# Six of the twelve pairs of layer-1 modulation tiles moved from the prompt attention into the first group of the sample attention

## The reference, cut to what matters

```python
def adaln(c, w, b):
    m = jax.nn.silu(c) @ w + b          # w: 1024 x 6144 per layer
    m = m.reshape(c.shape[0], 1, 6, D_MODEL)
    return [m[:, :, k] for k in range(6)]

def mla_sample(h, past_lat, past_rope, w_in, q_g, kv_g, w_qb, w_kvb, w_o):
...
    k_lat = jnp.concatenate([past_lat, ckv], axis=1)      # pages gathered by page_table
    k_pe = jnp.concatenate([past_rope, kr], axis=1)
    q = jnp.concatenate([q_lat, q_pe], axis=-1)
    k = jnp.concatenate([k_lat, k_pe], axis=-1)[:, :, None, :]
    o_lat = causal_attention(q, k, k_lat[:, :, None, :], t0)
```

## Time and profile before

| | before |
|---|---|
| median of 3 runs | 1791.84 us (1791.68 to 1793.46) |
| profiled execution: its own time, its span | 1792.22 us, 1790.4 us |
| TensorE busy; mean granted clock | 1670.3 us (93%); 0.966 |
| VectorE, ScalarE, GpSimd busy | 450.0, 266.8, 93.8 us |
| moved by DMA | 457.07 MB, mean 255 GB/s |
| prompt attention, first to last turning of probabilities | 177.35 to 252.57 us |
| sample attention, first cache transposition to output projection | 256.88 to 350.06 us |

### The profile page before, as it was taken

One profiled execution on the slowest core, in us unless ns is written; L12 is line 12 of the kernel. 1 busy time (PEld: TensorE's weight loads), 2 busy tenths in 40 slices (PEclk: granted clock), 3 DMA queues, 4 the chain that ended last, 5 costly groups with the idle time before them and its releaser, 6 DMA issues.

```text
span 1790.4 us, 21220 instructions
## 1 busy us (share of the span) xinstructions
PE 1670.3 (93%) x8202; PEld 1065.9 (60%) x8202; DVE 450.0 (25%) x1128; ACT 266.8 (15%) x564; POOL 93.8 (5%) x173
## 2 busy tenths in 40 slices
PE   6999997799999999987997999999999999999996
PEld 4555553478888878766774454554445544554454
DVE  2233432220000055698466000020000200020002
ACT  2222222110000022333312000010001000100002
POOL 0001415000000010100000000000000000000000
PEclk9998998899999999998998999999999999999998
DMA  9755963244434554544476699999999899989993
GB/s 339 263 205 170 335 227 109 82 130 142 153 111 129 184 187 123 146 130 125 134 285 239 229 360 390 385 360 363 380 385 382 294 383 392 383 301 369 383 387 139
DMA packets 253068, 457.07 MB, mean 255 GB/s; under 512 B 12959, under 2 KB 112316, under 8 KB 249861
## 3 DMA queue, kind: packets, MB, share of 16 engines
q1 hardware_dynamic: 240640, 413.03, 65.5%
q0 software_dynamic: 10224, 41.71, 6.7%
q10 hardware_dynamic: 2112, 1.05, 0.2%
HBM read 443.54 MB, written 12.40 MB: 255 GB/s over the span
## 4 chain that ended last, share of the span: by engine, by line
PE 84%; DVE 8%; DMA 3%; issue 2%; ACT 1%; SPq 1%; POOLq 0%; POOL 0%; DVEq 0%; ACTq 0%
PE bank L1261 17%; PE bank L974 9%; PE bank L1300 9%; PE bank L1276 9%; PE bank L947 7%; PE bank L1312 4%; PE bank L988 4%; PE bank L687 2%; DMA st<-in_state_ssm 2%; PE bank L1022 1%; PE bank L777 1%; PE bank L724 1%; DVE ysp L1907 1%; PE bank L695 1%; DVE prod L1906 1%
## 5 line engine op out<-in xcount | busy, mean ns | idle before, releaser
L1261 PE MATMUL bank<-ring,hg 128*128 128x512 f32 (+1 forms) x624 | 255.1, 566 | 0.0
L1261 PEld LDWEIGHTS bank<-ring,hg 128*128 128x128 f32 x624 | 118.7, 192 | 129.2 <-issue 126.7
L974 PE MATMUL bank<-hT,ring 128*128 128x264 f32 x704 | 156.9, 386 | 1.3 <-ACT hT L1397 1.3
L974 PEld LDWEIGHTS bank<-hT,ring 128*128 128x128 f32 x704 | 133.7, 190 | 24.9 <-issue 2.1
L947 PE MATMUL bank<-hT,ring 128*128 128x264 f32 x512 | 117.4, 390 | 1.7 <-ACT hT L1397 1.3
L1300 PE MATMUL bank<-ring,turnH 128*128 128x512 f32 x256 | 114.4, 599 | 2.7 <-ACT turnH L1610 2.7
L947 PEld LDWEIGHTS bank<-hT,ring 128*128 128x128 f32 x512 | 98.1, 192 | 19.6 <-issue 2.1
L2172 DVE TENSOR_TENSOR actH<-sgH,bank 128x512 f32<-128x512 f32 (+1 forms) x24 | 15.4, 641 | 374.2 <-PE bank L1261 374.2
L1276 PE MATMUL bank<-ringx,hg 128*64 128x256 f32 x832 | 93.0, 381 | 0.0
L1300 PEld LDWEIGHTS bank<-ring,turnH 128*128 128x128 f32 x256 | 47.2, 190 | 67.3 <-issue 63.6
L988 PE MATMUL bank<-actT,ring 128*128 128x264 f32 x352 | 79.1, 386 | 0.6 <-DVE actT L1810 0.6
(11 more groups left out here) (483 smaller groups left out, 1945.5 us busy)
## 6 DMA issues: line engine op xcount, KB each, us to landing
ring<-in_moe_w_down SPq DMA_DIRECT2D x70, 1024.0 KB, 10.6
ring<-in_moe_w_up SPq DMA_DIRECT2D x59, 1024.0 KB, 8.1
ring<-in_moe_w_gate SPq DMA_DIRECT2D x55, 1024.0 KB, 8.8
ring<-in_w_ada SPq DMA_DIRECT2D x48, 1024.0 KB, 8.5
ringx<-in_moe_w_gate SPq DMA_DIRECT2D x37, 1024.0 KB, 7.9
ringx<-in_moe_w_up SPq DMA_DIRECT2D x33, 1024.0 KB, 10.0
ring<-in_ssm_w_in SPq DMA_DIRECT2D x20, 1024.0 KB, 5.4
ringx<-in_moe_w_down SPq DMA_DIRECT2D x20, 1024.0 KB, 10.0
```

What stands on the lines that cost most here:

```text
L974: m = mm(bank[2 * w + q][:, 0:T], slot8(tl)[:, k, q * P:(q + 1) * P], hT[:, k, :], start=k == 0, stop=k == DC - 1)
L1261: m = mm(bank[b_][:, 0:width], hg[:, k, 0:CAPH], w[:, kk, :], start=k == 0, stop=k == DC - 1)
```

## The change

`ada1_pairs` spreads six pairs over the sixteen heads in place of twelve: heads 2, 5, 7, 10, 13 and 15 now have one. The pairs 6 to 11 are computed in the first group of samples by `ada1_late`, in sequences 0, 1 and 2, one behind the second and one behind the fourth set of latent transpositions. The last turning, and TensorE's wait for the addition into `mod`, stand behind sequence 3's transpositions, and VectorE's copies and its addition move accordingly. The scores against a sample's own key, 8 columns of `bank[2]`, move to columns 432 to 439, beside the modulation that is now still in that bank.

```diff
+ADA1_EARLY = 6
 def ada1_pairs(h):
-    return range(h * 12 // H, (h + 1) * 12 // H)
+    return range(h * ADA1_EARLY // H, (h + 1) * ADA1_EARLY // H)
...
-        ada1_turn(11)
         values(H - 1)
...
         pe.wait_ge(s["o_copied"], H // 2)
-        pe.wait_ge(s["ada_added"], 4)
+        def ada1_late(p):
+            ada1_turn(p - 1)
+            ada_partials(ADA1 + 2 * p, bank[3], 12 + p + (1 if p == ADA1_EARLY else 2))
...
                     m.then_inc(s["lat_turned"], 1)
+                    if b < 3 and n % 2:
+                        ada1_late(ADA1_EARLY + 2 * b + n // 2)
...
                     m.then_inc(s["rope_turned"], 1)
+                if b == 3:
+                    ada1_turn(11)
+                    pe.wait_ge(s["ada_added"], 4)
...
-                            out = bank[half][rows, 0:512] if half < 2 else bank[2][rows, 0:NB]
+                            out = bank[half][rows, 0:512] if half < 2 else bank[2][rows, 432:432 + NB]
...
-        v.wait_ge(s["ada_turned"], 24)
-        ada_add(1, bank[2][:, 0:432], 0, 48, 4)
...
+                if b < 3:
+                    for p in (ADA1_EARLY + 2 * b, ADA1_EARLY + 2 * b + 1):
+                        v.wait_ge(s["units"], unit(ADA1 + 2 * p + 1))
+                        v.tensor_copy(adaS[:, p % 2, :], bank[3][:]).then_inc(s["ada_copied"], 1)
...
+                if b == 3:
+                    v.wait_ge(s["ada_turned"], 24)
+                    ada_add(1, bank[2][:, 0:432], 0, 48, 4)
...
-            link(v.tensor_tensor(s8[:], bank[2][:, 0:NB], cst[:, C_SMASK + NB * g_:C_SMASK + NB * (g_ + 1)], ALU.add))
+            link(v.tensor_tensor(s8[:], bank[2][:, 432:432 + NB], cst[:, C_SMASK + NB * g_:C_SMASK + NB * (g_ + 1)], ALU.add))
```

## The result

The changed kernel is slower: 1821.53 us, the median of four runs (1817.56 to 1822.92), against 1792.16 for the kernel before; the ratio is 1.0155, with a 95% interval from 1.0138 to 1.0173, which is +27.8 us. The forecast was +18.2. Its profiled execution took 1821.71 us, 29.5 more than that of before.

A forecast was written before the change was run, and what follows sets the result against it. TensorE was taken as the bound, 84% of the chain. Prompt attention -6.0, first group +11.6, page wait +10.6 and cold clock +2.0 sum to +18.2 us: 1810.0 against the median, range 1802 to 1820.

The forecast's parts named there:

- the clock falling after head 3: Prompt attention: a sign of being wrong; the clock was to stay at 1.00 from head 3 on.
- The other two signs: Signs of being wrong: a wait before sequence 5 under 6 or over 14 us, or TensorE waiting for `w_ada` tiles.
- The first group, +11.6: Sequences 0 to 3: six pairs add 15.9 us, covered waits and low clock take off 5.5, the last turning adds 1.2.
- The pages, +10.6: Before sequence 5: page loops start after the late 24th turning, SyncE needs 34.5 us, so TensorE waits 10.6 us.
- The cold clock behind the wait, +2.0: Sequence 5: TensorE is cold after the page wait, costing 1.4 to 3.8 us, taken as 2.0.
- the sample attention as a whole: Sample attention: the first group, the page wait and the cold clock after it, forecast together at +24.2 us.
- The prompt attention, -6.0: Prompt attention: +0.5 for heads 0 to 2, -4.9 for five heads, -1.0 last turning, -0.6 addition into `mod`.
- the term of five heads, -4.9: Heads 2 to 15: five heads lose their pair, each lasting 4.24 in place of 5.22 us.
- The rival of the falling clock: Prompt attention: idle heads bring the clock down, +15 us if half are cold, +31 if all; 1825 to 1841; chance 0.06.
- Heads 0 to 2, +0.5: Head 0's turning to head 2's, at the low clock: -1.6 to +1.7 us without head 1's pair, taken as +0.5.

The follow-up runs named there:

- experiment 1: Kernel before, with the page loops for sequences 4 to 7 starting only when sequence 3's rotary rows are turned; 1807.38 us, ratio 1.0071.
- experiment 2: Changed kernel with the rotary pages of sequences 4 to 7 in the value tile, freed from the 24th turning; 1811.06 us, ratio 1.0076.
- experiment 11: Changed kernel with one matmul of 512 columns, its result unread, in heads 0 and 1 only; 1816.60 us, ratio 1.0121.

## Why the prediction was right, and where it was mis-sized

**The bound and the sign** were right: time in TensorE's stream came through one for one. The time also fell into the range, but that is partly luck. The prediction had named the clock falling after head 3 as a sign of being wrong, and it fell at 200 us, just behind head 4's turning. The other two signs stayed away: the wait was 13.7 us, within 6 to 14, and no tile of `w_ada` was waited for. The piece behind the output projection took 1437.6 to 1445.3 us in twelve of the thirteen profiles, and 1453.8 in one, without a trend with the change.

**The first group, +11.6:** measured +11.1. The six pairs, the wait and the low clock of sequence 3 that they cover, and the last turning went as worked out; the scores followed the 24th turning by 0.7 us, not 1.2.

**The pages, +10.6:** the mechanism was right (experiments 1 and 2) and the size 3.1 short. From the turning to TensorE's wake-up it took 37.6 us, not 36.3: 0.8 of that because I had taken the pace below that of before, for which there was no reason, and 0.5 for the last page's landing. TensorE came to sequence 5 in 23.1 us in place of 24.5, because the clock came back earlier in the product with the latent rows (4.99 us, before 6.54), and the scores were half a microsecond nearer to the turning. **The cold clock behind the wait, +2.0:** 1.6. These misses nearly cancel, since an earlier TensorE only waits longer: the sample attention as a whole was forecast at +24.2 and came to +25.1, and to +25.8 in the second profile of the changed kernel.

The Trainium skill, "DMA: Bandwidth & Descriptors", section "Issuing engines are not separate DMA queues", calls a sequencer's time to start a transfer usually small beside the transfer. The trace agrees on that: the long issuing instruction takes 0.35 us, and a page lands in about 2. The prediction had set the sentence against a whole round of the loop, 2.04 to 2.30 us, and that was the wrong comparison: two thirds of a round go to the page's number and the loop's own small instructions. The conclusion, that the loop and not the transfer sets the pace, stands all the same, by experiment 1.

**The prompt attention, -6.0: the step that failed is the term of five heads, -4.9.** It priced a head without a pair at 4.24 us and a head with one at 5.22, each right at the full clock, and let the clock stay full because single such heads had left it so. The clock didn't stay: the stretch came out above its 58.9 us by 9.4 in the first profile and by 11.1, 4.6 and 5.4 in the three others of that kind, so that it gained nothing on the whole. The rival of the falling clock, with a chance of 0.06, was therefore true at about half its middle price (+15), and on top of the forecast, not in its place. The sum 18.2 + 7.6 (the mean of the four) is 25.8. The touched pieces of the two profiles of the changed kernel add up to +26.5 and +23.6, and its two medians lie at +27.8 and +25.8. With the clock kept between heads 2 and 15 that stretch took 58.78 us, the forecast's value.

The Trainium skill, "TensorE: Matmul & The Clock Gate", section "A second HAM failure mode: psum-queue depth-cycling", says that brief idle spells between groups of matmuls, if frequent, make the clock swing. Here the trace agrees: in eight of thirteen heads TensorE idles 1.57 us of 4.21, there are low stretches in all four profiles, and there are none once 0.87 us of each spell is filled. I had named it and set it aside on three heads that stood alone, a case the section doesn't speak of.

**Heads 0 to 2, +0.5:** -1.3 in one profile and -0.2 in the second of the changed kernel (11.24 against 11.47); this varies with the clock. The prediction speaks of heads 0 and 1 at the low clock, but its row of 0.53 ends at head 1's turning; the next 5.22 us, up to head 2's, were already at 1.00.

**The range** 1802 to 1820 was stated against the first median; the measured +27.8 on that median is 1819.6, at its upper edge, and 1821.5 by the plain median is beyond it. It reached up only a little past the forecast because the falling clock was given 0.06; with more weight on it the end would have been 1825, where that rival began.

Still open: at which spacing of idle heads the clock begins to fall (one in four left it alone in two profiles of three); why the low stretches differ in number and length from one execution to the next; and whether it is the shorter idle spell or the added matmul that keeps the clock.

## What to carry to other kernels

Idle time that work leaves behind on TensorE isn't free even when the wait is another engine's: read how the clock stands in a stretch with as many gaps as the change will make, not in one with a single gap, and try a filler in the gaps. When work is moved to a later place, list what is released by its end, here two loops that issue for some 33 us, and compare with the slack that each had. A loop that issues small transfers has a duration of its own, which belongs in the sum like any instruction's; look inside one round before saying what it is made of.

## What the runs showed of the hardware that was not expected

The clock also fell while TensorE had no gap in its row: in the changed kernel at 244.6, with the engine busy since its last idle spell had ended at 242.66, and busy for 4.00 of 4 us in the window shown; a window's own busy share doesn't tell its clock. At the low clock the idle time that the softmax chain sets stays as it is (1.65 us in experiment 11 at 217.49, in place of 1.57), so that a low stretch costs less than twice: a head with a pair took 8.49 us in place of 5.22, and one without 5.79 in place of 4.21, its clock low for part of it. A float32 matmul of 512 columns with a weight of 128 by 128 takes 0.87 us, while the eight of a pair, whose weights are 128 by 32, take 1.85 together, 0.23 each. A filler of 0.87 us in head 0, put into a wait, shortened the two heads behind a cold start from 11.5 to 8.7 us.
